# Hybrid decoder step: the samples' selected branch loads only its 15 chosen cache blocks, two samples an item

## The reference

```python
cur = posi // SEL_BLOCK
valid = jsel[None, :] <= cur[:, None]
dist = cur[:, None] - jsel[None, :]
forced = (jsel[None, :] == 0) | ((dist >= 0) & (dist < N_LOCAL))
rank = jnp.where(valid, impi + BIG * forced.astype(jnp.float32), -BIG)
_, idx = lax.top_k(rank, k_top)          # k_top = 16
kvg = ks[bi, gi, idx].reshape(B, N_KV_B, qb, k_top * SEL_BLOCK, 2, HD_B)
```

## Time and profile before

| | us |
|---|---|
| median of 3 runs | 2640.61 |
| lowest and highest of them | 2637.81, 2641.68 |
| the profiled execution: own time | 2638.68 |
| its span in the trace | 2636.3 |
| mean granted TensorE clock | 0.994 of full speed |

### The profile page before, as it was taken

One profiled execution on the slowest core, in us unless ns is written; L12 is line 12 of the kernel. 1 busy time (PEld: TensorE's weight loads), 2 busy tenths in 40 slices (PEclk: granted clock), 3 DMA queues, 4 the chain that ended last, 5 costly groups with the idle time before them and its releaser, 6 DMA issues.

```text
span 2636.3 us, 51872 instructions
## 1 busy us (share of the span) xinstructions
PE 2572.9 (98%) x21479; PEld 2478.3 (94%) x21479; DVE 1501.9 (57%) x1952; ACT 939.1 (36%) x1631; POOL 1458.4 (55%) x948
## 2 busy tenths in 40 slices
PE   8999989999999999999999999999999999999998
PEld 8999978987787899999999999999999999999998
DVE  6112375877665227555576678345346554677676
ACT  4100034656667224333333333210134333333332
POOL 6332200112323367877798885543559777788881
PEclk9999999999999999999999999999999999999999
DMA  6112453351204623354464431311323434563431
GB/s 202 41 34 65 121 147 101 97 178 49 95 21 138 248 80 138 114 175 145 179 221 165 154 129 49 129 57 40 105 105 113 153 135 155 190 245 137 139 127 65
DMA packets 199266, 328.26 MB, mean 125 GB/s; under 512 B 11277, under 2 KB 126738, under 8 KB 195386
## 3 DMA queue, kind: packets, MB, share of 16 engines
q1 hardware_dynamic: 189712, 306.02, 34.3%
q0 software_dynamic: 2880, 10.49, 1.1%
q10 hardware_dynamic: 6442, 8.46, 1.0%
HBM read 233.22 MB, written 95.90 MB: 125 GB/s over the span
## 4 chain that ended last, share of the span: by engine, by line
PE 89%; DVE 5%; issue 2%; POOL 2%; ACT 1%; DMA 1%; SPq 0%; ACTq 0%; DVEq 0%; POOLq 0%
PE psum L957 21%; PE psum L933 21%; PE psum L484 16%; PE psum L532 7%; PE psum L976 3%; PE psum L2347 2%; PE psum L2814 2%; PE psum L2844 2%; PE psum L2340 1%; PE psum L520 1%; PE psum L2320 1%; PE psum L3713 1%; PE psum L2783 1%; PE psum L3396 1%; PE psum L562 1%
## 5 line engine op out<-in xcount | busy, mean ns | idle before, releaser
L957 PE MATMUL psum<-part_hi,whl 128*128 128x258 f32 x3136 | 507.8, 284 | 1.2 <-POOL whl L397 1.0
L957 PEld LDWEIGHTS psum<-part_hi,whl 128*128 128x128 f32 x3136 | 434.2, 189 | 1.9 <-POOL whl L397 1.4
L484 PE MATMUL psum<-xhi,whl 128*128 128x344 f32 x1776 | 329.2, 320 | 2.1 <-DVE qT L1676 1.0
L1240 DVE TENSOR_TENSOR xlo_plain<-xlo_plain,psum 128x516 f32<-128x516 f32 x360 | 245.2, 688 | 141.7 <-PE psum L957 139.3
L933 PE MATMUL psum<-shi,whl 128*128 128x258 f32 x1920 | 323.9, 283 | 0.0
L454 POOL TENSOR_TENSOR whl<-wraw,zeroc 128x1024 fp32r<-128x1024 f32 x62 | 120.4, 1942 | 357.4 <-PE psum L484 171.8
L957 PE MATMUL psum<-part_lo,whl 128*128 128x258 f32 x1568 | 315.0, 282 | 0.0
L484 PEld LDWEIGHTS psum<-xhi,whl 128*128 128x128 f32 x1776 | 288.2, 188 | 2.6 <-issue 2.6
L933 PEld LDWEIGHTS psum<-shi,whl 128*128 128x128 f32 x1920 | 271.5, 190 | 0.0
L933 PE MATMUL psum<-xhi,whl 128*128 128x258 f32 x1440 | 249.6, 285 | 4.1 <-POOL whl L365 4.1
L957 PEld LDWEIGHTS psum<-part_lo,whl 128*128 128x128 f32 x1568 | 243.2, 190 | 0.0
(11 more groups left out here) (532 smaller groups left out, 5249.3 us busy)
## 6 DMA issues: line engine op xcount, KB each, us to landing
part_raw<-b_spill SPq DMA_DIRECT2D x98, 516.0 KB
b_spill<-rows_H SPq DMA_DIRECT2D x78, 516.0 KB, 3.9
rows<-in_cache_cmp_kv SPq DMA_DIRECT2D x128, 128.0 KB, 2.6
raw_even<-in_w_ffn SPq DMA_DIRECT2D x16, 1024.0 KB, 5.9
out_even<-in_w_ffn SPq DMA_DIRECT2D x16, 1024.0 KB, 6.2
out_odd<-in_w_ffn SPq DMA_DIRECT2D x16, 1024.0 KB, 6.0
raw_odd<-in_w_ffn SPq DMA_DIRECT2D x14, 1024.0 KB, 6.9
wraw<-in_w_in_ab SPq DMA_DIRECT2D x26, 512.0 KB, 4.4
```

What stands on the lines that cost most here:

```text
L484: last = pe.matmul(psum[:, 3 * bset + c, 0:TC], w, rhs[ah][:, k0 + k, c * TC:(c + 1) * TC], start=(k == 0 and n == 0), stop=(k == kn - 1 a ...
L957: last = pe.matmul(psum[:, 2 * p + h, 0:QT], out_weights(first, n, wh)[:, k, p % 2, :], (part_hi, part_lo)[ah][x][:, k, h * QT:(h + 1) * Q ...
L1240: event(dve.tensor_tensor(quarters(out_total(i, p)), quarters(out_total(i, p)), two_banks(p), ALU.add))
```

## The change

- VectorE makes a list `chosen` for each of the 64 query rows (8 for each sample, four of a group alike): 13 numbers of chosen blocks in the cache, counted over the whole pool in blocks of 64 tokens, as integers. The page numbers of each sample are spread to its rows and made into block keys (`bkey`) in `dve_sample_masks`; `dve_block_choice` takes the chosen ones out with two maximum-of-eight operations.
- Rows are then loaded by block: for each sample and group 13 DMAs of one block's 64 tokens, keys and values of this group (`chosen_rows`), each at an address from a register load of `chosen`. The two forced blocks are loaded whole (`forced_rows`: 16 partitions of the first page, 32 of the last, of which the half that isn't forced is masked or overwritten). So a sample has two row tiles and not four, and an item holds two samples.
- `ITEMS` is s0, s1, w0, w1, s2, s3: six items and not ten. The mask of the one unused half block (`negs`) is added by two small products in TensorE; VectorE's `masked_scores` goes, and maximum and exponential read PSUM.
- The sample steps stand earlier among the prompt's jobs, so that the list is there earlier: steps 0 to 5 at tiles 2, 2, 3, 3, 4, 5, where they stood at 4, 4, 5, 5, 6, 7.
- SyncE loads samples 0 to 6 and GpSimd sample 7. SyncE's order: forced rows of 0 to 3, queries and gates, window rows 0, forced rows of 4, a wait for `chosen`, chosen rows of 0 to 4, forced rows of 5, window rows 1, chosen rows of 5, new rows 1, window rows 2 and 3, forced and chosen rows of 6, new rows 2 and 3, a wait for the value product of s1, the reload of `xhi` and `xlo`.
- The window rows have four buffers and not two. `other_branches` stands behind the values of the last item but one.

```diff
-        SAMPLE_STEPS = ((4, 5), (4, 9), (5, 4), (5, 8), (6, 6), (7, 7))
+        SAMPLE_STEPS = ((2, 3), (2, 7), (3, 5), (3, 8), (4, 5), (5, 3))
...
-        ITEMS = ("w0", "s0", "s1", "s2", "s3", "s4", "w1", "s5", "s6", "s7")
+        ITEMS = ("s0", "s1", "w0", "w1", "s2", "s3")
         LAST = len(ITEMS) - 1
-        BUFFER = (0, 1, 4, 5, 3, 2, 0, 1)
-        ROWS_IN = {1: 64, 2: CACHE_ROWS[1], 3: CACHE_ROWS[1], 4: 64, 5: 64, 6: 64, 7: 128}
+        DYNAMIC = 13
+        ROWS_IN = 2 * 16 * (2 * DYNAMIC + 2)
...
+        def forced_rows(eng, b):
+
+            first = eng.value_load(pt[0:1, 16 * b:16 * b + 1], min_val=0, max_val=table.shape[0] - 1)
+            last = eng.value_load(pt[0:1, 16 * b + 15:16 * b + 16], min_val=0, max_val=table.shape[0] - 1)
+            tiles = srows[b // 2][2 * (b % 2):2 * (b % 2) + 2]
+            eng.dma_start(tiles[0][0:16, :], rows_of_page[bass.ds(first, 1), 0:16, :].rearrange("n m c -> (n m) c"))\
+                .then_inc(rows_sem(b), 16)
+            eng.dma_start(tiles[1][96:128, :], rows_of_page[bass.ds(last, 1), :, :].rearrange("n m c -> (n m) c"))\
+                .then_inc(rows_sem(b), 16)
+
+        def chosen_rows(eng, b):
+
+            for g in range(2):
+                r = HB * b + 4 * g
+                for x in range(DYNAMIC):
+                    i, k = (0, x + 1) if x < 7 else (1, x - 7)
+                    block = eng.value_load(chosen[r:r + 1, x:x + 1])
+                    eng.dma_start(srows[b // 2][2 * (b % 2) + i][16 * k:16 * k + 16, :]
+                                  .rearrange("p (x g d) -> p x g d", g=2, d=64)[:, :, g, :],
+                                  blocks_of_table[bass.ds(block, 1), :, :, g, :].rearrange("n m x d -> (n m) x d"))\
+                        .then_inc(rows_sem(b), 16)
...
-            for b in (2, 3):
-                for i in range(4):
-                    for q, page in enumerate(page_numbers(sp, cache_sel[0], b, (2 * i, 2 * i + 1))):
-                        sp.dma_start(srows[BUFFER[b]][i][32 * q:32 * q + 32, :],
-                                     cache_sel[0][bass.ds(page, 1)].rearrange("n (m e) a g d -> (n m) (e a g d)", e=4))\
-                            .then_inc(m_rows[1], 16)
+            for b in range(4):
+                forced_rows(sp, b)
...
             sp.wait_ge(p_ea, step_done(2))
-            window_rows(1)
-            new_rows(1)
-            first_numbers = [page_numbers(sp, cache_sel[0], 0, (2 * i, 2 * i + 1)) for i in range(2)]
+            forced_rows(sp, 4)
+            sp.wait_ge(sD, DVE_S["chosen"])
+            for b in range(5):
+                chosen_rows(sp, b)
             sp.wait_ge(p_ql, 2 * NT)
             sp.wait_ge(p_qk, soft_no[job_no[("c", NT - 1, 0)]] + 1)
...
-            sp.wait_ge(sP, PE_S[f"V{place('w0')}"])
+            forced_rows(sp, 5)
+            sp.wait_ge(p_qk, soft_no[job_no[("s", NT - 1, HB - 1)]] + 1)
+            window_rows(1)
+            chosen_rows(sp, 5)
+            new_rows(1)
+            sp.wait_ge(p_qk, len(SOFT))
             window_rows(2)
             window_rows(3)
+            forced_rows(sp, 6)
+            chosen_rows(sp, 6)
             new_rows(2)
             new_rows(3)
-            sp.wait_ge(sP, PE_S[f"V{place('s3')}"])
+            sp.wait_ge(sP, PE_S[f"V{place('s1')}"])
...
         def pool_sample(pool):
-            pool.wait_ge(m_ix, 4)
+            pool.wait_ge(sD, DVE_S["chosen"])
             pool.wait_ge(p_qk, soft_no[job_no[("s", NT - 1, HB - 1)]] + 1)
-            gather(pool, cache_sel[0], srows[BUFFER[1]], 1, rows_sem(1))
...
+            forced_rows(pool, 7)
+            chosen_rows(pool, 7)
...
         def dve_block_choice(dve):
-            dve.tensor_scalar(selneg[:, :], rank[:, :], -1e29, NEG, ALU.is_gt, ALU.mult).then_inc(sD, 1)
+            chained(dve, dve.tensor_scalar(ckey[:, :], rank[:, 0:32], -1e29, None, ALU.is_lt))
+            chained(dve, dve.tensor_tensor(ckey[:, :], ckey[:, :], bkey[0:R, :], ALU.mult))
+            chained(dve, dve.max(top[:, 0, :], ckey[:, :]))
+            chained(dve, dve.match_replace(ckey[:, :], top[:, 0, :], ckey[:, :], -1.0))
+            chained(dve, dve.max(top[:, 1, :], ckey[:, :]))
+            dve.tensor_scalar(chosen[:, :], top[:, :, :].rearrange("r x y -> r (x y)"), -1.0, 1.0 / 64, ALU.add, ALU.mult)\
+                .then_inc(sD, 1)
...
-            sp.wait_ge(sP, PE_S[f"V{place('s4')}"])
+            sp.wait_ge(sP, PE_S["S0"])
             units = [wcols(w_out_ab[0], P * j, P) for j in range(8)]
...
-            pool.wait_ge(sP, PE_S[f"V{place('w1')}"])
+            pool.wait_ge(sP, PE_S[f"V{place('w0')}"])
             pool_split(pool, phases["ab_out"], 1)
```

More of the change, by code:

```diff
@@ L3144, in dve_selected @@
             for p in range(LAST + 1):
-                order += [f"ma{p}"] if selected(p) else []
+                order += ["ow", "ww"] if p == LAST else []
                 order += [f"pts{p - 1}"] if p else []
                 order += [f"mx{p}"]
-                order += ["osel0"] if p == 6 else ["ow", "ww"] if p == 7 else []
+                order += ["osel0"] if p == 4 else []
             return order + ["st", f"pts{LAST}"]
@@ L3152, in build @@
         ACT_S = steps("cmp", *act_selected(), "rowexp", "hi")
-        DVE_S = steps("gg", "pgz", "masks", "qe", "cmpmax", "pcs", "pgsel", "cmpw", "knz", "pre",
+        DVE_S = steps("gg", "pgz", "masks", "qe", "cmpmax", "pcs", "chosen", "cmpw", "knz", "pre",
                       *dve_selected(), "rowd", "osel1", "wrow", "wsel", "pnT", "osb", "lo")
@@ L3358, in pe_gate_spread @@
                 for i in range(4):
-                    pe.matmul(psum[32 * i:32 * i + 32, 3, 8 * half:8 * half + 8], ident[0:R, c],
-                              selneg[:, 8 * i:8 * i + 8], start=True, stop=True)
-                for i in range(4):
                     pe.matmul(psum[32 * i:32 * i + 32, 3, 16 + half:17 + half], ident[0:R, c], g64[:, 2:3],
@@ L3378, in pe_keys_back @@
             if selected(p):
-                x = BUFFER[n]
-                if i == 0 and n == 0:
-                    pe.wait_ge(m_rows[0], 128 * NB + 256)
-                elif i == 0:
-                    pe.wait_ge(rows_sem(n), ROWS_IN[n])
-                source = [srows[x][i][:, 256 * e:256 * e + P] for e in range(4)]
+                if i == 0:
+                    pe.wait_ge(s_sr[n], ROWS_IN if n < 3 else ROWS_IN // 2)
+                elif i == 2 and n == 3:
+                    pe.wait_ge(s_s7, ROWS_IN // 2)
+                source = [srows[n][i][:, 256 * e:256 * e + P] for e in range(4)]
             else:
@@ L3387, in pe_keys_back @@
                 pe.wait_ge(s_wr[b // 2], 32)
-                source = [wrow[(b // 2) % 2][:, b % 2, e, 0:P] for e in range(4)]
+                source = [wrow[b // 2][:, b % 2, e, 0:P] for e in range(4)]
             if p and i >= 2:
```

243 lines of the change are left out of this document (110 added, 133 removed).

## The result

| | before | after |
|---|---|---|
| time, median (range) | 2641.14 us (2637.81 to 2643.18, 4 runs) | 2690.14 us (2686.14 to 2693.20, 4 runs) |
| profiled execution: its time, span | 2638.7, 2636.3 | 2688.47, 2686.9 |
| first item's transposes, L484 | 838.05, 905.04 | 841.99, 955.26 |
| mean granted clock | 0.994 | 0.982 |

The ratio is 1.0186, with a 95% interval of 1.0168 to 1.0204: the change costs 49 us, clear of the noise. The forecast was 2652.7 with a range of 2624 to 2684.

What follows compares the result with a forecast made beforehand. TensorE was taken as the bound, made to wait by SyncE's issue of 182 loads: stage end 12.3 us later plus 1.7 for low clock, 14.0 in all; 2638.7 + 14.0 = 2652.7 us, range 2624 to 2684.

Steps and rivals of the forecast that it cites:

- What bounds the kernel: TensorE: busy 98% of the span, so only its lost work or waits count; cache bytes saved give nothing by themselves.
- What is removed: Sample stage: ten items become six, which takes away 4 x 4.49 = 18.0 us of TensorE.
- VectorE: Masks and choice: 20 small operations, at most 7 us of VectorE; charged nothing to 2 us, 0 taken; list ready at 702.
- SyncE's list: Sample stage: window item w1 waits for its new rows, issued behind 182 loads of chosen rows; TensorE waits 27 us.
- the price t: SyncE's time to issue one load of chosen rows: 0.92 us, between 0.78 and 1.16, with 0.42 for the DMA instruction.
- X: Sample stage: the time at which the new rows of w1 have landed, 702 + 167.4 + 9.8 = 879.2.
- Rival B: Chance 0.13: bounds check stays in each load, DMA instruction costs as for 2 KB pieces; t 1.06 to 1.16, 2680 to 2697.
- After w1: From X to the stage's end at L484: 38.1 us, with 3.6 us of wait for the reload; 1.7 added for low clock.
- A: Rival, 0.40 with the zone up to the crossing: t below 0.85, 2625.6 at 0.78. ("A grew": length, `xlo` to first transposes.).
- C: Rival, 0.05: GpSimd's loads of sample 7 end last; decides only if one costs over 2.6 us; at 3.5, 2679.
- D: Rival, 0.02: the list is ready later than the jobs say, about 20 us for each step missing its place; 2673.
- E: Rival, 0.01: a register load of a value VectorE has just written costs 0.6, not 0.27; t = 1.25, 2713.

Runs made afterwards that it cites:

- half the list: Changed kernel with one load per block for both groups (group 1 gets group 0's blocks), 91 SyncE loads for 182, new rows of w1 ahead of sample 6: 2633.9 us.
- the last two kernels: Changed kernel, loads shared evenly between SyncE and GpSimd, masks in idle time, reload in halves; GpSimd three a place, then two and four: 2630.4 and 2626.2 us.
- experiment 4: Changed kernel with another access pattern for each sample's loads, then patterns over 128 partitions; only the DMA instruction was read, not the time.
- t = 0.84: Changed kernel with the same 208 loads, each with 16 pieces of 2 KB in place of 128 of 256 bytes: 2648.1 us, ratio 1.0034.
- the kernel with t = 0.68: Changed kernel with the same 208 loads and pieces, but from fixed blocks, with no register load or address arithmetic: 2639.8 us, ratio 1.000.

## Why the prediction was wrong

It forecast 14 us more for the profiled execution, and 50 came. The sign was right, the step that failed is the price of one load, and two smaller terms were undersized.

**What bounds the kernel**, right: only TensorE's lost time counted, and no run shows a gain from the bytes saved.

**What is removed**, right: 18.0 us were forecast for four items. With half the list the stage is 11.3 us shorter, with 6.5 more in the wait for `whl`. In the last two kernels, where the reload goes in halves and that wait is 1.3 to 1.5, it is 17 us shorter.

**VectorE**, wrong: charged at nothing to 2 us, and 0 taken, "because the wait below absorbs it". Duration and slack were read as sums over a stretch, not at the place where the masks stand: in one piece of 4.1 us, where an average over a stretch, as in the earlier trace rows, says nothing. A grew by 4.4 us, of which the masks' place is 2.7 (239.1 against 241.8, with two low stretches of the clock in both); the other 1.7 go with the clock. In the changed kernel it counts through the list, ready at 704.3 and not at 702 (+2.3); with the wait gone it counts in full.

**SyncE's list**, the mechanism right: that the window item w1 waits for the new rows behind the 182 loads, released by the transfer from the key-value scratch, and that no selected row is waited for. The step that failed is the price t: the DMA instruction was put at 420 ns, between 368 and 469, and took 564; the other parts of t were met within 0.02 us. 182 x (1.077 - 0.92) = 28.6 us, most of the miss. With t and the list's time as measured, the working gives X = 704.3 + 182 x 1.077 + 9.8 = 910.1, and 910.7 was measured. The two rows were no bounds: the 469 is of one run of memory for each partition and the 368 of the weights' shape, and neither is 8 strided pieces in 16 partitions. By experiment 4 the stride in memory is 247 ns of the 564. The count of pieces, argued away, was rightly argued away; the conclusion that the third level costs little was not. Rival B had the size, 1.06 to 1.16, and its 2680 to 2697 took the result in, but by luck: the check, its reason, wasn't there, and the instruction cost more than its 469.

**After w1**, undersized: X to L484 was put at 38.1 + 1.7; it was 44.6, and 43.5 with half the list, where w1 doesn't wait at all. In the changed kernel the reload went out 6.6 us behind X, not 4.5 (eight transposes took 1.97 us there and 1.04 at full clock), the split began 15.5 later, not 13.6, and from the unit's start to L484 18.0 went, not 15.6. Of the 43.5 the reload and its weights took 15.8 to the split's start, and from the unit's start to L484 17.8 went. The clock accounts for the last step: in the last row below it was 0.58, behind 6.5 us without work. After the change it was 0.57 from 932 to 944. The forecast let it be low once, for a moment; each long wait brings its own stretch at 0.5 to 0.7, near the lower of the two levels (1.2 of 2.4 GHz). Two stretches with half the list:

```profile
872.00:882.00 10.00, 3.65 (x54) 3.34 (x54) 1.23 (x5) 0.78 (x2) 4.01 (x2) 0.74 0.59 189
882.00:888.00 6.00, 5.72 (x24) 5.66 (x25) 0.36 (x2) 0.00 (x0) 4.44 (x3) 0.58 0.32 94
```

The sum closes: 28.6 + 2.3 + 0.6 on X and 4.8 after it are 36.3, and L484 stands at 955.3 where the forecast had 919.0. The total of the profiled execution, 2688.5 against 2652.7, is off by 35.8.

**The rivals.** A needed t below 0.85: at t = 0.84 the time was 2648.1, not 2640, and the kernel with t = 0.68 is level (2639.8), since the masks and the clock had to be won back too. C was false as argued: GpSimd's loads took 0.94 us each, and 528 ns in the instruction, with VectorE busy for 15.8 of the 30 us from 820 to 850. The Trainium skill, "SBUF — State Buffer", section SBUF: two separate sides, has GpSimd's descriptors wait for VectorE's two-port operations; no row here shows it. Nor do the prediction's four gathers test it, as no row tells which of VectorE's operations beside them, 3.15 us of 6, is of that kind. D false, save for the 2.3 us. E false: a register load of a value just written took 273 ns, at most 291. **The range** ended at 2684. The measured price alone brings the forecast to 2681, still inside; the late list and what follows w1 take it out. No end of the range had either term larger. Two sums of the prediction are a little off: t = 1.0 gives 2667, not 2669, and B begins at 2678, not 2680; nothing hangs on them.

## What to carry to other kernels

Price a new DMA instruction by its pattern, on both sides, and take a row as a bound only if it has the same pattern: here two rows of others missed by 95 and 196 ns. A load issued one by one pays for its register and check besides. A transfer's time is the length of the queue ahead of it plus what each entry there waits for, so look for everything behind the list (here new rows and the reload), and cut the list into shares for the engines with idle time between their own operations. Small operations added to an engine with slack on average still stall the bound engine where they stand in one piece, and low stretches of the clock behind a wait belong in the sum.

## What the runs showed of the hardware that was not expected

- In the patterns tried here SyncE's DMA instruction takes 316 to 333 ns with one run of memory for each partition, whether it is 16 x 2 KB or 128 x 256 bytes, and 543 to 564 with two, four or eight strided pieces for each. Scatter on the chip's side adds nothing (317). Two other loads don't fit and stay open: 469 for 64 x 2 KB, one run each, and 368 for the weights' 8 strided pieces in each of 128 partitions.
- A register load from on-chip memory took 273 ns on SyncE and 300 on GpSimd; with the address's arithmetic and the gaps it is 0.40 us of a load. The bounds check adds 0.27.
- GpSimd issues the same load every 0.94 us, faster than SyncE with 1.08, and its instruction takes 528 ns.
- After the wait of 26 us TensorE worked at a granted clock of 0.50 for all of the 3.8 us that it had work, and after that of 28 us at 0.68 over 8 us (1.00 from 918 on). In the prompt attention a wait of 2.7 us was followed by 0.57 over 4 us in some kernels, and in others, with the same waits, by none.
